# Rotary embedding of a streaming encoder's queries: a second product or an exchange of lanes

## The reference

```python
def _rope(x, pos):
    half = x.shape[-1] // 2
    ...
    x1 = x[..., :half].astype(jnp.float32)
    x2 = x[..., half:].astype(jnp.float32)
    return jnp.concatenate([x1 * cos - x2 * sin, x2 * cos + x1 * sin], axis=-1).astype(x.dtype)

q_lat, kv_lat, kpe_raw, dq, dk, dv = jnp.split(h @ w_in, SPLIT_EVEN, axis=-1)
q = (_rmsnorm(q_lat, g_q_lora) @ w_q_up).reshape(b, s, MLA_HEADS, MLA_NOPE + MLA_ROPE)
q_nope, q_pe = q[..., :MLA_NOPE], _rope(q[..., MLA_NOPE:], pos)
ckv = _rmsnorm(kv_lat, g_kv_lora)
kpe = _rope(kpe_raw, pos)
```

## Time and profile before

| | us |
|---|---|
| median of three runs | 1674.75 (1674.34 to 1675.99) |
| profiled execution | 1674.04 |
| its span, first to last instruction | 1672.2 |
| TensorE busy | 1639.2 (98%) |
| VectorE busy | 1105.0 (66%) |
| ScalarE busy | 804.4 (48%) |
| GpSimd busy | 576.6 (34%) |
| mean granted TensorE clock | 0.998 |

### The profile page before, as it was taken

One profiled execution on the slowest core, in us unless ns is written; L12 is line 12 of the kernel. 1 busy time (PEld: TensorE's weight loads), 2 busy tenths in 40 slices (PEclk: granted clock), 3 DMA queues, 4 the chain that ended last, 5 costly groups with the idle time before them and its releaser, 6 DMA issues.

```text
span 1672.2 us, 31609 instructions
## 1 busy us (share of the span) xinstructions
PE 1639.2 (98%) x12240; PEld 1589.7 (95%) x12248; DVE 1105.0 (66%) x2047; ACT 804.4 (48%) x1502; POOL 576.6 (34%) x432
## 2 busy tenths in 40 slices
PE   9999999999999999999999999999999999999998
PEld 8989999999998999999999999899989999999998
DVE  5666655555655996587477689533358965874876
ACT  4465555454655654255144445545456541551443
POOL 4453446454553032022013357655550320220122
PEclk9999999999999999999999999999999999999999
DMA  7221223334323133233233322443241332332231
GB/s 193 77 62 53 59 76 98 79 96 108 81 63 80 52 102 114 64 101 104 74 90 88 86 68 69 118 114 89 58 116 52 101 106 71 100 103 76 77 100 58
DMA packets 282744, 145.45 MB, mean 87 GB/s; under 512 B 60334, under 2 KB 273004, under 8 KB 282596
## 3 DMA queue, kind: packets, MB, share of 16 engines
q1 hardware_dynamic: 278136, 136.27, 29.5%
q0 software_dynamic: 3616, 6.92, 1.6%
q10 hardware_dynamic: 844, 0.24, 0.1%
HBM read 130.69 MB, written 15.32 MB: 87 GB/s over the span
## 4 chain that ended last, share of the span: by engine, by line
PE 81%; DVE 11%; ACT 3%; issue 3%; DMA 1%; POOL 1%; SPq 0%; DVEq 0%; ACTq 0%
PE ACC L1269 39%; PE ACC L1682 7%; PE ACC L1684 7%; PE ACC L1683 7%; PE T L1269 3%; PE S L1269 2%; PE ACC L1549 2%; PE S L1524 2%; DVE SCO L2863 2%; DVE TOP L2860 1%; ACT PR L2114 1%; PE S L1684 1%; PE S L1682 1%; PE S L1683 1%; PE T L1537 1%
## 5 line engine op out<-in xcount | busy, mean ns | idle before, releaser
L3502 POOL TENSOR_TENSOR HF<-SG,U 128x576 f32<-128x576 f32 x44 | 65.1, 1478 | 498.4 <-ACT SG L2302 402.3
L1269 PE MATMUL ACC<-XGh,WH 128*128 128x288 f32 (+1 forms) x1008 | 227.6, 307 | 6.7 <-ACT U L2367 2.2
L3347 POOL TENSOR_TENSOR WL<-RAW,WH 128x1024 fp32r<-128x1024 f32 (+3 forms) x84 | 181.4, 2162 | 147.5 <-ACT WH L1989 147.2
L1269 PE MATMUL ACC<-XGh,WL 128*128 128x288 f32 (+1 forms) x1008 | 215.4, 295 | 0.0
L1269 PE MATMUL ACC<-XGl,WH 128*128 128x288 f32 (+1 forms) x1008 | 215.4, 295 | 0.0
L1989 ACT ACTIVATE WH<-RAW 128x1024 fp32r<-128x1024 f32 (+3 forms) x159 | 153.2, 971 | 79.6 <-PE ACC L1269 43.4
L1682 PE MATMUL ACC<-TB,WH 128*128 128x288 f32 x640 | 189.1, 295 | 0.6
L1684 PE MATMUL ACC<-TB,WL 128*128 128x288 f32 x640 | 188.8, 295 | 0.0
L1683 PE MATMUL ACC<-TB,WH 128*128 128x288 f32 x640 | 188.4, 294 | 0.0
L1269 PE MATMUL ACC<-HH,WH 128*128 128x288 f32 x1032 | 179.2, 295 | 0.0
L1269 PEld LDWEIGHTS ACC<-XGh,WH 128*128 128x128 f32 (+1 forms) x1008 | 159.2, 188 | 11.8 <-issue 3.2
(11 more groups left out here) (469 smaller groups left out, 4308.3 us busy)
## 6 DMA issues: line engine op xcount, KB each, us to landing
RAW<-in_w_gate_dram SPq DMA_DIRECT2D x44, 512.0 KB, 3.9
RAW<-in_w_up_dram SPq DMA_DIRECT2D x44, 512.0 KB, 4.6
RAW<-in_w_down_dram SPq DMA_DIRECT2D x32, 512.0 KB, 4.1
RAW<-in_w_in_even_dram SPq DMA_DIRECT2D x29, 512.0 KB, 5.0
RAW<-in_w_in_odd_dram SPq DMA_DIRECT2D x28, 512.0 KB, 4.4
RAW<-in_w_out_even_dram SPq DMA_DIRECT2D x16, 512.0 KB, 4.0
RAW<-in_w_down_dram SPq DMA_DIRECT2D x16, 384.0 KB, 3.5
RAW<-in_w_out_odd_dram SPq DMA_DIRECT2D x8, 512.0 KB, 5.2
```

The source lines that it names most:

```text
L1269: ins = pe.matmul(out[0:m, 512 * b:512 * b + width], left, right[:, b * width:(b + 1) * width], start=(first and part == 0), stop=(last an ...
L3347: pool.tensor_tensor(WL[slot][:, 0:n], RAW[slot][:, 0:n], WH[slot][:, 0:n].bitcast(F32), ALU.subtract).then_inc(w_lo_pool, 1)
L3502: pool.tensor_tensor(HF[:, q, :], SG[:, q, :], U[:, q, :], ALU.mult).then_inc(h_out, 1)
```

## The change

The exchange of halves is done by VectorE's shuffle, which permutes lanes inside each square of 32 partitions. For that the channels lie otherwise: each 32 partitions hold 16 channels of the first half and the 16 that belong to them of the second. Weights, COS, SIN and the cached key are loaded in this order by more, smaller DMAs (SP: 12 for a pe unit instead of 9; 8 for COS and SIN instead of 2; 4 for the cached key instead of 2; 2 for the key weights instead of 3). The kp unit is permuted while it is split, in two instructions on ScalarE and on VectorE. Key outputs are put back in order by a permuted identity (IDP), made by two VectorE copies.

The product "ps" is gone. Behind "pe" VectorE multiplies by COS into SBUF and shuffles the accumulator in place; one slot later it multiplies by SIN in place and adds (`finish_rotation`). The value product of head 2 moves from slot 4 of head 1 to slot 3; the queries of head 3 move from slot 0 of head 2 to slot 7 of head 1; output tile 4 in heads 3 and 5 moves from slot 2 to slot 4; in the prologue two latent tiles instead of three are turned before head 0.

```diff
+HALF_SWAP = [(i + SQUARE // 2) % SQUARE for i in range(SQUARE)]
-LATENT_TILES = {2: 4, 5: 5, 6: 6, 7: 7}
+LATENT_TILES = {4: 4, 5: 5, 6: 6, 7: 7}
-    "even": [("q", 0, 3), ("k", 0, 2), ("v", 0, 2), ("pe", 0, 3), ("ps", 0, 3), None, None, None],
+    "even": [("q", 0, 3), ("k", 0, 2), ("v", 0, 2), ("pe", 0, 3), None, None, None, None],
-    "first even": [("q", 0, 3), ("k", 0, 2), ("pe", 0, 3), ("ps", 0, 3), ("v", 0, 2), None, None, None],
+    "first even": [("q", 0, 3), ("k", 0, 2), ("pe", 0, 3), ("v", 0, 2), None, None, None, None],
+    if (h, s) == (1, 7):
+        return 3, "q", 0, QLT, QLT
-    if g is None or (h, s) == (1, 0):
+    if g is None or (h, s) in ((1, 0), (2, 0)):
-            for n, w in enumerate(("k", "v", "pe", "ps", "q")):
+            for n, w in enumerate(("k", "v", "pe", "q")):
-    EARLY_LATS = 3
+    EARLY_LATS = 2
...
+                        for h in range(2):
+                            first = (name[1] + h) * (HD + ROPE) + HD
+                            pe = halves_apart(wq[k * P:(k + 1) * P, first:first + ROPE])
+                            for q in range(2):
+                                dst = raw[:, k * P + h * ROPE + q * SQUARE:k * P + h * ROPE + (q + 1) * SQUARE]
+                                sp.dma_start(dst, pe[:, q]).then_inc(loaded, 16)
...
                 prepare(g, "pe", 0, QLT)
-                prepare(g, "ps", 0, QLT)
                 prepare(g, "q", 0, QLT)
...
+            def exchange_halves(out, dst):
+                dve.tensor_tensor(two(dst), halves(out), two(COS[:, :]), ALU.mult)
+                link(dve.stream_shuffle(halves(out), halves(out), HALF_SWAP))
+            def add_exchanged(out, dst):
+                link(dve.tensor_tensor(halves(out), halves(out), two(SIN[:, :]), ALU.mult))
+                return dve.tensor_tensor(two(dst), halves(out), two(dst), ALU.add)
+            def finish_rotation(g):
+                add_exchanged(pair(acc.at("pe", g)), rotated(g)).then_inc(acc_free, 1)
...
-            dve.tensor_tensor(two(YQ[lower, :]), halves(TT)[lower], two(COS[lower, :]), ALU.mult)
-            link(dve.tensor_tensor(two(YK[lower, 0:NT]), halves(TT)[upper], two(SIN[upper, :]), ALU.mult))
-            link(dve.tensor_tensor(YQ[lower, :], YQ[lower, :], YK[lower, 0:NT], ALU.add))
-            dve.tensor_tensor(BO[lower, 0, :], YQ[lower, :], RSTD[lower, :], ALU.mult).then_inc(kp_taken, 1)
-            dve.tensor_tensor(BO[upper, 0, :], YQ[lower, :], RSTD[lower, :], ALU.mult).then_inc(lat_ready, 1)
+            exchange_halves(TT, YQ)
+            add_exchanged(TT, YQ).then_inc(kp_taken, 1)
+            dve.wait_ge(kp_taken, 1)
+            dve.tensor_tensor(BO[:, 0, :], YQ[:, :], RSTD[:, :], ALU.mult).then_inc(lat_ready, 1)
...
                     elif what == "pe":
-                        ins = dve.tensor_tensor(two(rotated(g)), halves(out), two(COS[:, :]), ALU.mult)
-                    elif what == "ps":
-                        link(dve.tensor_tensor(halves(out), halves(out), two(SIN[:, :]), ALU.mult))
-                        dve.wait_ge(acc_free, acc.made("pe", g))
-                        ins = dve.tensor_tensor(two(rotated(g)), halves(out), two(rotated(g)), ALU.add)
+                        exchange_halves(out, rotated(g))
+                        return
...
+                    if s and share(h, s - 1) and share(h, s - 1)[1] == "pe":
+                        finish_rotation(g)
                     if c and c[3] == c[4] and s < 7 and not (h == 16 and c[1] == "k" or h == 0 and c[1] == "v" or keys_early(h, s)):
                         write_projection(c[0], c[1])
...
                 dve.memset(KPLE[ROPE:P, :].bitcast(F32), 0.0)
-                write_projection(g, "ps")
+                finish_rotation(g)
                 begin("q", g)
```

More of the change, by code:

```diff
@@ L341, in plan_attention @@
                 r, what, k0, k1, total = c
-                if k0 == 0 and what not in ("v", "ps") or (k0 == 0 and what == "v" and kind_of(r) != "mla"):
+                if k0 == 0 and what != "v" or (k0 == 0 and what == "v" and kind_of(r) != "mla"):
                     if kind_of(r) != "mla":
@@ L349, in plan_attention @@
                     else:
-                        unit("pe", r, cols=2 * QLT * P, end=("ps", r), in_slot=True)
+                        unit("pe", r, cols=QLT * P, end=("pe", r), in_slot=True)
                 if k1 == total:
@@ L682, in build @@
         (COS, SIN), end = overlay(second, ("COS", [P, NT], F32), ("SIN", [P, NT], F32))
-        (MASK,), end = overlay(end, ("MASK", [P, SEQ], BF16))
+        (MASK, IDP), end = overlay(end, ("MASK", [P, SEQ], BF16), ("IDP", [P, P], F32))
         assert end <= cursor[0]
@@ L845, in last_s, with halves_apart, rotary_columns @@
             return sc.made("s", h, TOK_TILES - 1, 1 if kind_of(h) == "diff" else 0)
+        def halves_apart(rows):
+            return rows.rearrange("p (s q i) -> p q s i", s=2, q=2)
+        def rotary_columns(tile, turned=False):
+            order = "p (m q s i) -> p m q s i" if turned else "p (m s q i) -> p m q s i"
+            return tile[:, :].rearrange(order, q=2, s=2, i=SQUARE // 2)
         def rows_of(t):
@@ L924, in unit_loads @@
                 if w == "kp":
-                    c, r = Q_LORA + KV_LORA, ROPE // 2
-                    return [(0, ROPE, tiles(w_even, 0, DT, c, ROPE)), (ROPE, r, tiles(w_even, 0, DT, c + r, r)),
-                            (ROPE + r, r, tiles(w_even, 0, DT, c, r))]
+                    return [(o, ROPE, tiles(w_even, 0, DT, Q_LORA + KV_LORA, ROPE)) for o in (0, ROPE)]
                 if w == "qi":
@@ L1444, in prepare @@
                     latent_product(("q", g), ("q", g), 0, P, k0, k1, QLT, QGh, QGl, HALF)
-                elif what in ("pe", "ps"):
-                    latent_product((what, g), ("pe", g), 0 if what == "pe" else QLT * P, P, k0, k1, QLT, QGh, QGl, HALF)
+                elif what == "pe":
+                    latent_product(("pe", g), ("pe", g), 0, P, k0, k1, QLT, QGh, QGl, HALF)
                 else:
@@ L2531, in unit_lo @@
                 slot = slot_of[name]
+                if name == ("kp",):
+                    old, new, high = rotary_columns(RAW[slot]), rotary_columns(WL[slot], turned=True), rotary_columns(WH[slot], turned=True)
+                    dve.tensor_tensor(new[:, :, 0], old[:, :, 0], high[:, :, 0].bitcast(F32), ALU.subtract)
+                    dve.tensor_tensor(new[:, :, 1], old[:, :, 1], high[:, :, 1].bitcast(F32), ALU.subtract).then_inc(w_lo, 1)
+                    return
                 dve.tensor_tensor(WL[slot][:, 0:n], RAW[slot][:, 0:n], WH[slot][:, 0:n].bitcast(F32),
@@ L2592, in query_latent_lo @@
                                          in1=QGh[:, i, :].bitcast(F32), op0=ALU.mult, op1=ALU.subtract).then_inc(qg_lo, 1)
+            def exchange_halves(out, dst):
[6 more added lines that the diff above has]
+                add_exchanged(pair(acc.at("pe", g)), rotated(g)).then_inc(acc_free, 1)
             dve.wait_ge(id_in, 16)
             link(dve.tensor_scalar(IDB[:, :], IDN[:, :], BIG, None, ALU.mult))
+            for h in range(2):
+                dve.tensor_copy(rotary_columns(IDP)[:, :, h], rotary_columns(IDN, turned=True)[:, :, h]).then_inc(idp_made, 1)
             take_x(0)
```

51 lines of the change are left out of this document (26 added, 25 removed).

## The result

| | before | after |
|---|---|---|
| median of 5 runs, us | 1674.75 | 1681.41 |
| lowest to highest, us | 1674.34 to 1675.99 | 1680.64 to 1683.23 |
| profiled execution, us (its span) | 1674.04 (1672.2) | 1683.23 (1681.4) |
| mean granted clock of TensorE, share of full speed | 0.998 | 0.994 |

The ratio is 1.0035, 95% interval 1.0024 to 1.0046: slower by more than the 0.2% that count here. The time lies outside the range. Single runs of the kernel before get this long too: of its 95 runs beside the experiments six took 1680.7 to 1681.8 us, at a mean granted clock of 0.994 to 0.996, and the others at most 1678.8.

A forecast was written before the change was run, and what follows sets the result against it. TensorE, busy 98%, bounds the kernel, but its saved 9.84 us turn into waits for VectorE: -0.2 -0.2 +1.1 = +0.7 on the profiled 1674.04, which lies 0.7 under the median, so 1675.4; range 1671 to 1679.

The forecast's parts named there:

- the sum: Whole kernel: gains and losses of order and waits added to +0.7 us on the profiled 1674.04, forecast 1675.4.
- E: Rival: clock falls behind new waits of 2.5 to 3.3 us in heads 1, 3, 5; +4.8 us, 1680; chance 0.03.
- The ceiling: Heads 0, 2, 4, 6: four removed "ps" products of 18 matmuls, 2.46 us each, at most 9.84 us gained.
- rival B: TensorE decides after all, tile 5 and turnings find data ready: 1665, or 1670 with half kept; together 0.17.
- The shuffle: VectorE, each product: one 128x576 shuffle in PSUM takes 0.77 us, 0.79 with the wait behind it.
- rival C: The shuffle is dear, in four chains ending on VectorE; at two passes 1678.5 us; chance 0.11.
- Heads 3 and 5: Tile 5 waits for VectorE to evacuate tile 4, weight split 2.1 us beside GpSimd: loss 0.55 per head, 1.1 together.
- Nothing gives it back: Heads 3 and 5: all behind tile 5 is TensorE's, so the 0.55 us lost per head is not recovered.
- Prologue and head 0: Head 1's queries wait for head 0's accumulator pair; gain 0.2 us, between gain 1.1 and loss 0.3.
- A first difference before 60 us: Sign that the forecast is wrong: the runs before and after already differ ahead of 60 us.
- Head 1 and 2: Stall of some 3 us at turning tile 4, head 3's queries cover a 0.48 gap: gain 0.2, bounds 1.0 either way.
- The sum of the order: Prologue and head 0 -0.2, heads 1 and 2 -0.2, heads 3 and 5 +1.1, the rest nothing: +0.7 us.

The follow-up runs named there:

- short fillers: Changed kernel plus 7, 9 and 11 throw-away matmuls in TensorE's four waits (prologue, head 1, heads 3 and 5); median 1676.34, ratio 1.0003 to the kernel before.
- the edit at 541.59: Kernel before, with the first half of output tile 2 computed a second time in TensorE's wait of 1.17 us; 1674.53, ratio 0.9994.

## Why the prediction was wrong, step by step

**The step that failed is the clock, which the sum put at nothing** and the rivals held as E, with a chance of 0.03 and 4.8 us (1.6 for each of three waits). The sum prices a wait of TensorE at its own length and leaves the matmuls behind it their full speed. The split of the 9.19 us between the two profiled executions, with the short fillers (1676.68) as the kernel after at a full clock: 2.64 us are order and waits, 6.55 are the clock. The profiled execution after is the slowest of its five; by the ratios the split is 0.0003 and 0.0032 of 0.0035, so the clock's share is 5.4 us. The mean clocks of the two, 0.994 and 0.999, differ by 0.005 of 1681 us: some 8 us of full clock were withheld (an estimate), a part of them while TensorE stood. The clock's part by stages, after less short fillers: 0.3 in head 0, 2.65 in head 3, 1.36 in head 5, 1.3 behind head 7 (1.4 by the two waits around the stretch at 549), and 0.87 ahead of head 0's first scores, of which 0.17 is no clock but a later start of the whole run (TensorE goes on behind its wait for the squares at 65.45 for 65.28). E itself was mis-sized in two ways: it saw heads 1, 3 and 5, while the clock also fell in the prologue and behind a wait that the change doesn't touch; and in head 1 it did not fall. The ground for 0.03 was a 9 for the clock in every slice and no wait over 1.4 us. The row of slices reads the same after, where the clock fell four times, so it can't rule a short fall out; and it is no evidence against a fall behind 3 us: no row showed what a wait of that length does. A cost outside the rows should have had its bound in the range, and with 1680 in it the range would have reached the rival, if not quite the 1681.41 that came.

**The ceiling, and rival B.** Right. The 72 matmuls came off TensorE, and all of their 9.84 us and more turned into waits: 2.25, 0.94, 2.69, 3.02 and 3.30 (12.2 together), at the named places with the named releasers.

**The shuffle, and rival C.** Right. Forecast 0.77 and 0.79 to the next start; measured 0.76 and 0.79. VectorE's timeline after, head 3, answers to the earlier trace rows:
```profile
148.81 2.25 DVE L2554 TENSOR_TENSOR WL<-RAW,WH 128x1024 fp32r<-128x1024 f32 x1
150.98 0.68 DVE L2824 CUSTOM_DVE_ANT_0 SX<-S,MASK 128x512 f32<-128x512 f32 x1
...
153.38 0.01 DVE L2619 LOAD_MASK_SELECT ACC<-ACC  x1
153.38 0.76 DVE L2619 STREAM_SHUFFLE ACC<-ACC 128x576 f32<-128x576 f32 x1
154.17 0.35 DVE L2821 TENSOR_SCALAR_CACHE_REDUCE SX<-S 64x192 f32<-64x192 f32 x1
...
155.29 0.74 DVE L2623 TENSOR_TENSOR ACC<-ACC,SIN 128x576 f32<-128x576 f32 x1
156.06 0.76 DVE L2624 TENSOR_TENSOR YQ<-ACC,YQ 128x576 f32<-128x576 f32 x1
156.73 0.75 DVE L2570 TENSOR_TENSOR X<-ACC,X 128x576 f32<-128x576 f32 x1
```
**Heads 3 and 5.** The mechanism was right, and the size held at a full clock: the chain from tile 3's minimum to tile 5 is 157.54-150.98 = 6.56 (forecast 6.61), and the heads take 0.57 and 0.86 longer with short fillers (forecast 0.55 each). The split takes 2.25, with GpSimd at work from 148.56 to 149.98 across it, and head 5's takes 2.27 with GpSimd at 198.87 to 200.29; forecast 2.1. The Trainium skill ("GPSIMD Engine Reference", its table of the engine's basics) says that a VectorE instruction with two SBUF inputs contends with GpSimd; both traces agree, 2.44 and 2.25 beside GpSimd against 1.22. "Nothing gives it back" was too strong: heads 4 and 6 are 0.33 and 0.40 shorter.

**Prologue and head 0.** The first scores came at 79.76 in a run that was 0.48 late by 65 us, so at 79.28 for the 79.21 forecast. (That lateness is not the change's: at the same matmul the other versions are anywhere from 64.66 to 65.57, and the kernel before with only the edit at 541.59 is at 65.19. "A first difference before 60 us", a sign of being wrong, can't be told from this spread.) Head 0's end was 0.6 late by the same measure, not 0.2 early: the last latent tile waited 0.94 for VectorE, and the key product followed 0.4 later than before instead of 0.2.

**Head 1 and 2.** Forecast a gain of 0.2; none came, 40.60 at a full clock against 40.59. The turning of tile 4 came 18.33 behind the head's first scores, 18.19 before; the second scores of head 2 21.47 behind it, 22.10 before. That is the gain that the queries' move was to give. It was gone by the end of head 2, and its place is the wait of 0.71 for VectorE's YK at 124.58, which the forecast took as hidden.

**The sum of the order.** +0.7 forecast. The ratio 1.0003 is +0.5 us, with an interval of 3.3 us; the profiled pair says +2.6. Of these 0.48 are the late start and 0.9 lie behind head 7, both within the spread of profiles that differ in nothing there. What is left is +1.3: +0.6 to the end of head 0 (forecast -0.2), nothing in heads 1 and 2 (-0.2), +1.4 in heads 3 and 5 (+1.1), and -0.7 in heads 4 and 6 (nothing). So the forecast of the order stands within what can be told, with head 0 mis-sized by 0.8, and it is the clock that put the time outside.

## What to carry to other kernels

Before pricing a new wait of TensorE at its own length, ask what it does to the clock behind it: where TensorE is the bound, a few us of idle time can cost a good part of their length again in slower matmuls (2.65 us behind a wait of 3.02, 1.36 behind one of 3.30). If the profile has no wait of that length, the price is unknown and its bound belongs in the range. Read it from the clock column of narrow windows and the number of matmuls in them, not from the busy share; and test it with fillers that end before the wait does, since fillers that outlast it cost what they should have shown.

## What the runs showed of the hardware

- One and the same wait is followed by a lowered clock in one run and not in another. In profiles where it was not filled: 1.17 or 1.18 us near 545, lowered in four of twelve; 2.25 in the prologue, lowered in two of five; 2.69 in head 1, in two of four; 1.89 or 1.90 there, in none of two; 2.65 or 2.66, in one of two; 3.02 to 3.31, in six of six. So below 3 us the length alone does not decide. A second wait of 1.09 to 1.21 us, near 578 (574.31 before, 583.52 after), has a full clock behind it in all fourteen profiles. What TensorE did before the two differs. Ahead of the one near 545 it ran ten matmuls of a single column, six of 288 and five of 128 (545.38 to 548.21 after); the last fifteen pairs ahead of the other are all of 288 columns. Whether that decides was not tested.
- The loss behind one such wait, after against short fillers, was 2.65 us in head 3, 1.36 in head 5 and 1.4 behind 549. It goes with how long the clock stays down (3.4 us of clock missing in head 3, 1.7 in head 5), and with waits of the same lengths the longer loss fell to head 3 in one version and to head 5 in another.
- Throw-away matmuls that fill most of a wait kept the clock full behind each wait that they filled, in six profiles; the repeated half of a tile did the same near 541 in two. Where they ended before the wait did, they cost nothing measurable: tile 5 of heads 3 and 5 began within 0.02 us of where it did without them.
- The exchange of lanes within groups of 32 took VectorE 0.76 us for 128x576 in PSUM, as long as the multiplication and the addition of that size beside it (0.74 and 0.76), and loading its mask 0.01.
